# Queries and keys turned by DMA transposes of the sync queue in place of TensorE transposes, in a hybrid transformer block

## The chip, the core and the metric

The kernel runs on one core of a Trainium2 chip. The metric is the device time of one execution in microseconds (us); the median of three executions of the kernel before is 1248.1 us. PE is TensorE, ACT is ScalarE, DVE is VectorE, POOL is GpSimd and SP is the sync engine, whose queue issues all of this kernel's transfers.

## What is computed

One transformer block works on 1024 latent tokens (a grid of 16 x 64) and 256 context tokens, all of width 1024. A modulated norm is projected, and the columns go to three mixers: a Hyena long convolution, grouped-query attention (GQA: 8 query heads, 2 key heads) and neighbourhood attention (4 heads, windows of 8 x 16). An output projection and a SwiGLU network follow. The change touches what lies between the projection and the two attentions:

```python
q_l = apply_rope(rms_norm(q_l, qk_g_q[l]), cos, sin)
k_l = apply_rope(rms_norm(k_l, qk_g_k[l]), cos, sin)
k_c = rms_norm(k_c, qk_g_k[l])
gqa_l = gqa_latent(q_l, jnp.concatenate([k_c, k_l], axis=1),
                   jnp.concatenate([v_c, v_l], axis=1))
na_l = natten_latent(nq_l, nk_l, nv_l, nk_c, nv_c, na_rpb[l])
```

## The kernel before

The kernel is written by hand: five instruction streams, one for each engine, tied by semaphores. Nothing reorders them, so the order in the code is the order on each engine, and a wait holds back everything behind it on that engine. Precise products are made of fp16 pairs: a value is split into a high part (written by ACT) and a low part (written by DVE or POOL), and three matmuls stand for one.

The projection for attention is cut into 28 units of 128 tokens. Units 0 to 9 (group 2) give the neighbourhood keys and values of the 8 latent and 2 context tiles. Units 10 to 19 (group 1) give the GQA keys and values of the 2 context tiles (10, 11) and of the 8 latent tiles (12 to 19); the latter also give the neighbourhood queries. Units 20 to 27 (group 0) give the GQA queries Q of the 8 latent tiles.

A unit u of group 1 goes this way: PE projects it (`project`, 24 matmuls of 512 columns); ACT squares and copies (`from_psum`); DVE sums; POOL takes the inverse root (`inverse_roots`); DVE scales and rotates; ACT writes the high parts into the staging tile `stk[u % 2]` (`hi_parts`), DVE the low parts (semaphore `pr_lo`); then PE turns the staging tile into PSUM, one 128 x 128 transpose for each head (`turn_qk`), and ACT copies the turned tile from PSUM to its home (`turned`, semaphore `pr_tc`). Keys go to `kT`, Q to `qT`; the neighbourhood queries are dealt into blocks of 8 rows x 16 columns in `nqT` by two copies. PE turns unit u - 2 right behind the projection of unit u.

From unit 19 on, neighbourhood attention runs in 32 iterations k (4 heads x 8 query blocks): `scores(k)`, `weigh(k - 2)`, `turn_p(k - 1)` (five fp32 transposes of probabilities) and a quarter of the projection of one Q unit (6 matmuls, `project_q`). In one of four iterations PE also turns a Q unit (8 transposes). `scores(0)` needs the blocked queries of units 12 to 15, `scores(4)` those of 16 to 19. The last Q unit, 27, is turned in GQA, six steps after its start. In some iterations a `chunk` of early GQA scores (512 columns) is added.

SP loads, in this stretch, copies of the neighbourhood values within SBUF (`load_near`, four DMAs of 128 KB each time, 2 then 0 and 1 then 3), bias pieces of 512 KB (`load_bias`), the gates and the next weights.

Of the kernel before, what the change touches and what calls it, by code (L numbers as in the profile page):

```python
# [14 lines left out]
P = 128  # L15
# [320 lines left out]
NKT = NT + NC  # L336
# [3 lines left out]
CATCH_UP, TURN_AT = (3, 6), 5  # L340
# [60 lines left out]
def build(nc, io, cst, lay, out):  # L401
    ctx = ExitStack()
    with ctx:
# [111 lines left out]
        nkT = f16(Z + 67, HN, 2, S + C)  # L515
        nT = [f32(o, 512) for o in (Z + 49, Z + 51)]
# [116 lines left out]
        pr_tc = sem("qk_transposed_copied")  # L633
        near_in = [sem("near_values_in"), sem("last_near_values_in")]
# [105 lines left out]
        def turned_bank(u):  # L740
            if u == NU - 1:
                return OUT_BANK[1]
            if u == GROUP0[0] - 1:
                return turned_bank(u - 1)
            return ((5, 4), (4, 3), (2, 3))[UNITS[u][0]][u % 2]

        def work(u):
            return u % 2

# [129 lines left out]
        def _(sp):  # L879
# [75 lines left out]

            sp.wait_ge(late_used, 2 * CHUNKS.count("late"))
            sp.wait_ge(pr_vl, n_valued(GROUP0[1] - 1))
            load_near(2)
            for n in range(BIAS_EARLY):
                load_bias(n)  # L960
            sp.wait_ge(split_lo, n_split(chunk_index("qkv", 5)))
            for cw in range(2):
                load_near(cw)
            sp.wait_ge(pr_r, n_normed(GROUP0[0] - 1))
            load_near(3)
            sp.wait_ge(pr_mm, GROUP0[0])
# [10 lines left out]
            for n in range(BIAS_EARLY + BIAS_RING, 3 * HN):  # L977
                load_bias(n)
# [141 lines left out]
        def _(pool):  # L1120
# [68 lines left out]

            def rotate_q(u):  # L1190
# [19 lines left out]
            for u in range(GROUP0[1], GROUP0[0]):  # L1210
# [7 lines left out]
                inverse_roots(u)  # L1218
            own.step(pool.memset(shifts, 0.0))
            for u in range(GROUP0[0], NU):  # L1220
# [5 lines left out]
                if u == GROUP0[0] + 2:  # L1226
                    pool.wait_ge(pr_tc, GROUP0[0] + 1)
# [97 lines left out]
        def _(pe):  # L1325
# [241 lines left out]
            def project_q(u, i):  # L1567
# [4 lines left out]
                elif i == 0:  # L1572
                    pe.wait_ge(pr_tc, u - 1)
# [5 lines left out]
            def turn_qk(u):  # L1579

                g, t = UNITS[u]
                pe.wait_ge(pr_lo, u + 1)
                if u == GROUP0[0] - 1:
                    pe.wait_ge(pr_tc, u)
                elif u >= 2:
                    pe.wait_ge(pr_tc, u - 1)
                if u == NU - 1:
                    pe.wait_ge(o_rdy, NNA)
                elif u > GROUP0[0]:
                    pe.wait_ge(s_max, max(n_chunked(Step(n)) for n, k in EARLY.items() if free_bank(k)[0] == u))  # L1590
                out16 = PS[:, turned_bank(u), :].bitcast(F16)
                for j in range(4 if g == 1 and t >= NT else 8):
# [15 lines left out]
            for u in range(2, GROUP0[0] - 1):  # L1608
# [10 lines left out]
                turn_qk(u - 2)  # L1619
# [56 lines left out]
            def chunk(c):  # L1676
# [11 lines left out]
                elif c.s == len(EARLY) + 1:  # L1688
                    pe.wait_ge(pr_tc, NU - 1)
# [1896 lines left out]
```

## Time and profile before

| what | value |
|---|---|
| times of three executions | 1247.28, 1248.1, 1249.35 us |
| span of the profiled execution | 1246.6 us |
| PE busy | 1226.5 us (98%) |
| DVE, ACT, POOL busy | 979.6, 653.0, 398.3 us |
| granted clock of TensorE, mean | 0.998 |
| projection of the units of group 1 | about 229 to 281 us from the span's start |
| iterations of neighbourhood attention | about 271 to 383 us |
| GQA | up to about 550 us |

The span is the time from the first to the last instruction of the profiled execution. It lies 0.7 to 2.8 us under the timed executions, which hold the launch too; the profiled execution has no other time of its own. A matmul's end is modelled, so the start of the next one tells more than a busy share.

### The profile page before, as it was taken

Reading aid. Unit: us, or ns where it says so; the run is one execution under the profiler, and the core shown is the slowest. Engines: PE = TensorE matmul, PEld = TensorE weight load, DVE = VectorE, ACT = ScalarE, POOL = GpSimd, SP = SyncE. Lnnn points to the kernel's source line nnn. Section 1 sums busy time; section 2 is a strip of 40 time slices with the busy share of each in tenths; the row PEclk is TensorE's granted clock in tenths of the full one; section 3 lists DMA queues with packets and bytes.
Section 4 is the critical chain, followed back from the end, with each engine's and each line's share of the span. In section 5 each row is a group of like instructions: output and inputs, shape, how many; then the busy total and the mean of one; then the engine's idle time right before and its main releaser. Section 6 shows DMA issues by size and latency. Waiting matters only on the chain. (4 is left out here: it accounts for less than half of the span.)

```text
span 1246.6 us, 22702 instructions
## 1 busy us (share of the span) xinstructions
PE 1226.5 (98%) x8085; PEld 668.1 (54%) x8085; DVE 979.6 (79%) x1597; ACT 653.0 (52%) x1231; POOL 398.3 (32%) x385
## 2 busy tenths in 40 slices
PE   7999999999999999999999999999999999999998
PEld 1564656556775666664454555554555554444444
DVE  3879998676778999964479888888888885666587
ACT  2642234556779999963145554455555543412425
POOL 0000000114678988850320444445554430000001
PEclk9999999999999999999999999999999999999999
DMA  9728723235210130121300332322223307997963
GB/s 354 282 87 318 260 78 136 68 87 155 67 35 2 35 136 9 29 86 51 118 34 1 102 102 84 92 85 66 87 90 101 101 28 265 336 339 249 351 228 135
DMA packets 111043, 164.35 MB, mean 132 GB/s; under 512 B 8560, under 2 KB 70000, under 8 KB 109552
## 3 DMA queue, kind: packets, MB, share of 16 engines
q1 hardware_dynamic: 110960, 163.24, 38.5%
q8 instruction: 52, 0.85, 0.3%
q14 instruction: 31, 0.25, 0.1%
HBM read 138.57 MB, written 22.55 MB: 129 GB/s over the span
## 5 line engine op out<-in xcount | busy, mean ns | idle before, releaser
L1327 PE MATMUL PS<-arena 128*128 128x512 f16 (+9 forms) x7485 | 1185.2, 319 | 13.1 <-DMA arena<-in_w_mod 5.7
L1327 PEld LDWEIGHTS PS<-arena 128*128 128x128 f16 (+3 forms) x7485 | 617.3, 100 | 555.3 <-issue 33.5
L3133 DVE SCALAR_TENSOR_TENSOR arena<-arena 128x512 f16<-128x512 f32 x128 | 111.6, 878 | 30.6 <-ACT arena L2361 29.8
L2361 ACT ACTIVATE arena<-arena 128x512 f16<-128x512 f32 x120 | 75.4, 631 | 103.2 <-PE PS L1327 103.2
L2491 ACT ACTIVATE arena<-arena 128x512 f16<-128x512 f32 x77 | 48.1, 629 | 124.7 <-DVE arena L3354 74.6
L3017 DVE TENSOR_REDUCE arena<-PS 128x1 f32<-128x512 f32 (+1 forms) x160 | 106.8, 680 | 3.3 <-PE PS L1327 3.3
L1321 POOL TENSOR_TENSOR arena<-arena 128x1 f32<-128x1 f32 x8 | 4.7, 598 | 231.3 <-DVE arena L3521 227.9
L2262 ACT ACTIVATE arena<-PS 128x512 f16<-128x512 f32 x125 | 75.7, 605 | 2.8 <-PE PS L1327 1.8
L1171 POOL TENSOR_TENSOR arena<-arena 128x512 f16<-128x512 f32 x64 | 74.0, 1158 | 8.0 <-ACT arena L2265 5.4
L3190 DVE TENSOR_TENSOR arena<-PS,arena 128x256 f32<-128x256 f32 (+1 forms) x100 | 55.2, 553 | 25.9 <-PE PS L1327 25.6
L3369 DVE SCALAR_TENSOR_TENSOR arena<-arena 128x512 f16<-128x512 f32 x77 | 52.2, 687 | 18.9 <-ACT arena L2491 18.8
L3041 DVE TENSOR_TENSOR arena<-PS,arena 128x512 f16<-128x512 f32 x96 | 65.3, 680 | 1.1 <-ACT PS L2265 0.9
L1297 POOL TENSOR_TENSOR arena<-arena 128x256 f32<-128x256 f32 x10 | 7.3, 726 | 183.7 <-DMA arena<-in_w_ffn_in 183.7
L3354 DVE TENSOR_TENSOR arena<-arena 128x512 f32<-128x512 f32 x44 | 30.2, 691 | 38.6 <-DMA arena<-in_w_ffn_out 33.3
L2436 ACT CAST arena<-arena 128x512 f16<-128x512 f32 (+1 forms) x77 | 45.2, 613 | 29.1 <-DVE arena L3239 17.4
L3253 DVE TENSOR_TENSOR arena<-arena 128x512 f16<-128x512 f32 (+1 forms) x77 | 60.3, 807 | 0.0
L2265 ACT ACTIVATE PS<-PS 128x512 f32<-128x512 f32 x96 | 57.9, 603 | 0.6 <-PE PS L1327 0.6
L1213 POOL MEMSET arena<- 128x128 f16 x2 | 0.4, 205 | 162.4 <-PE PS L1593 162.4
L2406 ACT COPY arena<-PS 128x512 f32<-128x512 f32 x60 | 33.9, 581 | 34.6 <-DVE arena L3253 18.8
L3142 DVE SCALAR_TENSOR_TENSOR arena<-arena 128x512 f16<-128x512 f32 (+2 forms) x30 | 41.6, 1414 | 0.0
L1187 POOL TENSOR_TENSOR arena<-arena 128x2 f32<-128x2 f32 (+1 forms) x18 | 20.3, 1126 | 61.8 <-DVE arena L2870 61.8
L2987 DVE CUSTOM_DVE_ANT_0 PS<-PS,arena 128x640 f32<-128x640 f32 x32 | 26.6, 831 | 17.1 <-PE PS L1327 17.1
(227 smaller groups left out, 1321.0 us busy)
## 6 DMA issues: line engine op xcount, KB each, us to landing
arena<-in_w_ffn_out SPq DMA_DIRECT2D x121, 256.0 KB, 5.2
arena<-in_w_mod SPq DMA_DIRECT2D x23, 1024.0 KB, 7.2
arena<-in_w_ffn_in SPq DMA_DIRECT2D x88, 256.0 KB, 3.0
left_operands<-arena SPq DMA_DIRECT2D x43, 256.0 KB, 2.9
arena<-in_w_in SPq DMA_DIRECT2D x9, 1024.0 KB, 5.6
arena<-left_operands SPq DMA_DIRECT2D x3, 2816.0 KB, 12.1
arena<-lay_bias SPq DMA_DIRECT2D x12, 512.0 KB, 3.9
arena<-in_x SPq DMA_DIRECT2D x2, 2048.0 KB, 14.1
```

The costliest lines, as they stand in the source:

```text
L1171: pool.tensor_tensor(pt[:, 1], Pf[s.full], pt[:, 0], ALU.subtract).then_inc(pt_lo2, 1)
L1327: return pe.matmul(out, lhsT, rhs, start=start, stop=stop, skip_group_check=True)
L2262: act.activation(Pt[s.s % RING_P][:, 0], PS[:, s.bank], ACT.Exp)
L2265: act.activation(Pf[s.full] if s.by_pool else PS[:, s.bank], PS[:, s.bank], ACT.Exp).then_inc(s_exp, 1)
L2361: act.activation(block_split(p, b)[:, 0], weight_block(p, b, first), ACT.Copy, scale=WS).then_inc(blk_hi, 1)
L2491: act.activation(foS[q % FO_RING][:, 0], src, ACT.Copy, scale=WS).then_inc(fo_hi, 1)
L3017: dve.tensor_reduce(out, ps, AX, ALU.max).then_inc(s_max, 1)
L3041: dve.tensor_tensor(pt[:, 1], PS[:, s.bank], pt[:, 0], ALU.subtract).then_inc(pt_lo, 1)
L3133: dve.scalar_tensor_tensor(dst[:, 1], src, WS, dst[:, 0], ALU.mult, ALU.subtract).then_inc(blk_lo, 1)
L3190: dve.tensor_tensor(buf, psum, buf, ALU.add).then_inc(fi_sum, 1)
L3253: dve.tensor_tensor(dst[:, 1], f_op[name], dst[:, 0], ALU.subtract).then_inc(fi_lo, 1)
L3369: dve.scalar_tensor_tensor(foS[q % FO_RING][:, 1], src, WS, foS[q % FO_RING][:, 0], ALU.mult, ALU.subtract).then_inc(fo_lo, 1)
```

## The change

Units 10 to 27 are no longer turned by PE. SP issues a DMA transpose from the staging tile for each: one of [128 x 512] for the keys of a unit of group 1, a second one of [128 x 512] for its neighbourhood queries (units 12 to 19), one of [128 x 1024] for a Q unit. Keys and Q land in `kT` and `qT` at once, without a copy by ACT. The neighbourhood queries land in one staging tile `nq_rows`, and POOL deals them into `nqT` by two copies (`block_queries`). Completion is counted on two semaphores used earlier for loads, `cols_in` and `rest_in`, by the parity of the unit. `pr_tc` now counts `turned` of units 0 to 9 and then `block_queries`. Units 0 to 9 are turned by PE as before.

```diff
+            def turn_qk(u):
+
+                g, t = UNITS[u]
+                sp.wait_ge(pr_lo, u + 1)
+                done = qk_in[u % 2]
+                if g == 0:
+                    sp.dma_start_transpose(qT[:, :, tok(t)], stk[work(u)]).then_inc(done, 16)
+                    return
+                keys = kT.rearrange("p h a s -> p (h a) s")
+                sp.dma_start_transpose(keys[:, :, tok(t)], stk[work(u)][:, 0:512]).then_inc(done, 16)
+                if t < NT:
+                    if t:
+                        sp.wait_ge(pr_tc, u - 2)
+                    sp.dma_start_transpose(nq_rows, stk[work(u)][:, 512:1024]).then_inc(done, 16)
...
-            for n in range(BIAS_EARLY + BIAS_RING, 3 * HN):
-                load_bias(n)
+            pieces = {BiasPiece(n - BIAS_RING).units_done: n for n in range(BIAS_EARLY + BIAS_RING, 3 * HN)}
+            for v in range(NNA):
+                if v % 4 == 3 and v > 3:
+                    turn_qk(GROUP0[0] + v // 4 - 1)
+                if v in pieces:
+                    load_bias(pieces[v])
+            turn_qk(NU - 1)
...
+            def block_queries(u):
+
+                t = UNITS[u][1]
+                pool.wait_ge(*qk_turned(u))
+                for r in range(2):
...
+                    ins = pool.tensor_copy(dst, nq_rows[:, :, GRID_W * r:GRID_W * r + GRID_W]
+                                           .rearrange("p h (b c) -> p h b c", b=4))
+                ins.then_inc(pr_tc, 1)
...
                 inverse_roots(u)
+                if u - 2 >= GROUP0[1] + NC:
+                    block_queries(u - 2)
...
-                elif i == 0:
-                    pe.wait_ge(pr_tc, u - 1)
+                elif i == 0 and u >= GROUP0[0] + 2:
+                    pe.wait_ge(pr_n, n_normed(u - 2))
...
                 project(u)
-                turn_qk(u - 2)
+                if u - 2 < GROUP0[1]:
+                    turn_qk(u - 2)
...
-            pe.wait_ge(pr_tc, GROUP0[1] + NC + NT // 2)
+            pe.wait_ge(pr_tc, GROUP0[1] + NT // 2)
             scores(Unit(0))
...
                 if k == 4:
-                    pe.wait_ge(pr_tc, first)
+                    pe.wait_ge(pr_tc, GROUP0[1] + NT)
...
-                if q_unit(k, 5) is not None:
-                    turn_qk(q_unit(k, 5))
...
-                if u >= 2:
+                if u >= GROUP0[1] + 2:
+                    act.wait_ge(*qk_turned(u - 2))
+                elif u >= 2:
...
-            if s == TURN_AT + 1:
-                turned(NU - 1)
```

How it moves the SP queue between the end of the weight loads and the gates. Before, `32x4x512` is one DMA of a near load and `lay_bias` a bias piece:

```order
L945 DMA arena<-arena 32x4x512 [waits values_lo,late_product_added]
L945 DMA arena<-arena 32x4x512 x3
L953 DMA arena<-lay_bias 128x1024 x2
L945 DMA arena<-arena 32x4x512 [waits split_lo]
L945 DMA arena<-arena 32x4x512 x7
L945 DMA arena<-arena 32x4x512 [waits qk_rotated]
L945 DMA arena<-arena 32x4x512 x3
```

The same stretch of the change, from the key transpose of unit 13 (its first row) to the keys of unit 17:

```order
L972 DMA_TRANSPOSE arena<-arena 128x4x128 [waits qk_lo]
L976 DMA_TRANSPOSE arena<-arena 128x4x128 [waits qk_transposed_copied]
L952 DMA arena<-arena 32x4x512 [waits values_lo,late_product_added]
L952 DMA arena<-arena 32x4x512 x3
L960 DMA arena<-lay_bias 128x1024 x2
L972 DMA_TRANSPOSE arena<-arena 128x4x128 [waits qk_lo]
L976 DMA_TRANSPOSE arena<-arena 128x4x128 [waits qk_transposed_copied]
L972 DMA_TRANSPOSE arena<-arena 128x4x128 [waits qk_lo]
L976 DMA_TRANSPOSE arena<-arena 128x4x128 [waits qk_transposed_copied]
L952 DMA arena<-arena 32x4x512 [waits split_lo]
L952 DMA arena<-arena 32x4x512 x7
L972 DMA_TRANSPOSE arena<-arena 128x4x128 [waits qk_lo]
```

The two transposes of units 14 and 15 stand between the near loads, those of units 16 to 18 behind the second batch, those of unit 19 behind the last; each second one (L976) waits for POOL to have emptied `nq_rows`.

On POOL, before, the inverse roots of units 12 to 19 (L1187) stand in a row, then a memset of `shifts` and the root of unit 20:

```order
L1216 MEMSET arena 128x16
L1216 MEMSET arena 128x4
L1187 TENSOR_TENSOR arena<-arena 128x2 [waits qk_mean_square,pool_steps] x8
L1219 MEMSET arena 128x512
L1187 TENSOR_TENSOR arena<-arena 128x8 [waits qk_mean_square]
```

The change, from the root of unit 18 on (L1222 is the root, L1233 the blocking copies, `columns_in` and `rest_in` the completion of a transpose of an even and of an odd unit):

```order
L1222 TENSOR_TENSOR arena<-arena 128x2 [waits qk_mean_square,pool_steps]
L1233 COPY arena<-arena 128x4x4x16 [waits columns_in]
L1233 COPY arena<-arena 128x4x4x16
L1222 TENSOR_TENSOR arena<-arena 128x2 [waits qk_mean_square,pool_steps]
L1233 COPY arena<-arena 128x4x4x16 [waits rest_in]
L1233 COPY arena<-arena 128x4x4x16
L1233 COPY arena<-arena 128x4x4x16 [waits columns_in]
L1233 COPY arena<-arena 128x4x4x16
L1233 COPY arena<-arena 128x4x4x16 [waits rest_in]
L1233 COPY arena<-arena 128x4x4x16
L1271 MEMSET arena 128x512 [waits qk_transposed_copied]
```

From the root of unit 14 on, each root is followed by a wait for the transfer of the unit two before and its two copies (unit 16 behind the root of 18), and the last root by those of units 17, 18 and 19.

## Rows read from the trace of the kernel before

**Rows 1.** The page: busy time of the engines, and TensorE's granted clock by slices.
```profile
PE 1226.5 (98%) x8085; PEld 668.1 (54%) x8085; DVE 979.6 (79%) x1597; ACT 653.0 (52%) x1231; POOL 398.3 (32%) x385
PEclk9999999999999999999999999999999999999999
```
**Rows 2.** Windows: length; PE, PEld, DVE, ACT, POOL busy us; clock; DMA share; GB/s.
```profile
230.00:281.00 51.00, 50.92 (x314) 26.90 (x312) 33.06 (x104) 27.90 (x75) 6.89 (x12) 1.00 0.28 78
299.00:375.00 76.00, 75.35 (x838) 53.21 (x835) 57.69 (x151) 57.06 (x140) 51.62 (x45) 1.00 0.21 67
387.00:430.00 43.00, 41.69 (x509) 27.36 (x507) 40.89 (x73) 42.59 (x85) 35.87 (x43) 1.00 0.09 26
```
**Rows 3.** Timeline of PE in group 1 (start, length, operation): projections and turns.
```profile
234.49 0.39 PE L1593 MATMUL PS<-arena 128*128 128x128 f16 x4
234.72 5.34 PE L1327 MATMUL PS<-arena 128*128 128x512 f16 x24
...
256.55 0.61 PE L1593 MATMUL PS<-arena 128*128 128x128 f16 x8
257.00 5.34 PE L1327 MATMUL PS<-arena 128*128 128x512 f16 x24
262.18 0.61 PE L1593 MATMUL PS<-arena 128*128 128x128 f16 x8
...
281.14 0.62 PE L1593 MATMUL PS<-arena 128*128 128x128 f16 x8 [0.22 <-DVE arena L2923]
```
**Rows 4.** Timeline of PE, one period of four near iterations.
```profile
299.23 0.61 PE L1593 MATMUL PS<-arena 128*128 128x128 f16 x8
...
303.24 0.74 PE L1656 MATMUL PS<-arena 128*128 128x128 f32 x5
303.81 2.66 PE L1327 MATMUL PS<-arena 128*128 128x512 f16 x28
306.31 0.74 PE L1656 MATMUL PS<-arena 128*128 128x128 f32 x5
...
311.81 0.61 PE L1593 MATMUL PS<-arena 128*128 128x128 f16 x8
```
**Rows 5.** Timeline of PE, near iterations with neither turn nor chunk.
```profile
283.44 0.72 PE L1656 MATMUL PS<-arena 128*128 128x128 f32 x5
284.00 2.44 PE L1327 MATMUL PS<-arena 128*128 128x512 f16 x27
286.28 0.74 PE L1656 MATMUL PS<-arena 128*128 128x128 f32 x5
```
**Rows 6.** Timeline of ACT at the start of GQA.
```profile
387.62 1.02 ACT L2170 COPY arena<-PS 128x1024 f16<-128x1024 f16 x1
```
**Rows 7.** Timeline of SP's issues, merged: near loads and bias pieces.
```profile
255.84 2.70 SPq L945 DMA_DIRECT2D arena<-arena  x4
258.59 1.07 SPq L953 DMA_DIRECT2D arena<-lay_bias  x2
262.17 5.13 SPq L945 DMA_DIRECT2D arena<-arena  x8
...
278.98 2.52 SPq L945 DMA_DIRECT2D arena<-arena  x4
```
**Rows 8.** The line of the near loads: issue ns, and us from issue to landing.
```profile
L945 SPq DMA_DIRECT2D arena<-arena x16: 586/604/750, 255.8 to 280.9; - x16
...
DMA to landing us min/median/max: 2.3/2.4/2.5
```
**Rows 9.** Copies like the blocking: lines of POOL and ACT, ns min/median/max.
```profile
L1159 POOL COPY arena<-arena x16: 601/604/609, 323.0 to 530.7; 64x512 f16<-64x512 f16 x16
L1213 POOL MEMSET arena<- x2: 205/205/205, 226.5 to 229.5; 128x128 f16 x2
L2185 ACT COPY arena<-PS x16: 372/384/490, 249.0 to 282.5; 128x256 f16<-128x256 f16 x16
```
**Rows 10.** Timeline of the weight loads of PE before `scores(4)`.
```profile
288.40 1.05 PEld L1327 LDWEIGHTS PS<-arena 128*128 128x128 f16 x21 [0.58 <-issue]
```
**Rows 11.** Timeline of PE and ACT at the longest pause of this stretch.
```profile
294.67 0.77 ACT L2239 ACTIVATE arena<-PS 128x384 f16<-128x384 f32 x2 [1.15 <-remote]
295.81 1.16 PE L1327 MATMUL PS<-arena 128*128 128x384 f16 x21 [1.50 <-issue]
```

More of the change, by code:

```diff
@@ L339 @@
 LEAD, LAG, SHIFT_AT, SEND_AT = 13, 4, 8, 4
-CATCH_UP, TURN_AT = (3, 6), 5
+CATCH_UP = (3, 6)
 RING_P, RING_F = 5, 4
@@ L515, in build @@
         nkT = f16(Z + 67, HN, 2, S + C)
+        nq_rows = f16(101.5, HN, P)
         nT = [f32(o, 512) for o in (Z + 49, Z + 51)]
@@ L740, in turned_bank, with has_q, qk_turned @@
         def turned_bank(u):
[L741 to L745, printed above, removed]
+            return 2 + u % 2
         def work(u):
             return u % 2
+        def has_q(u):
+            g, t = UNITS[u]
+            return g == 0 or (g == 1 and t < NT)
+        def qk_turned(u):
+            n = sum(2 if UNITS[v][0] == 1 and has_q(v) else 1 for v in range(GROUP0[1], u + 1) if v % 2 == u % 2)
+            return qk_in[u % 2], (16, N_REST)[u % 2] + 16 * n
         def q_unit(k, after):
@@ L954, in load_bias @@
                     .then_inc(bias_in[piece.slot], 16)
+            def turn_qk(u):
+                g, t = UNITS[u]
+                sp.wait_ge(pr_lo, u + 1)
[9 more added lines that the diff above has]
+                    sp.dma_start_transpose(nq_rows, stk[work(u)][:, 512:1024]).then_inc(done, 16)
+            sp.wait_ge(y_rdy, 4)
+            for u in range(GROUP0[1], GROUP0[1] + 4):
+                turn_qk(u)
             sp.wait_ge(late_used, 2 * CHUNKS.count("late"))
@@ L960, in _ @@
                 load_bias(n)
+            for u in range(GROUP0[1] + 4, GROUP0[1] + 6):
+                turn_qk(u)
             sp.wait_ge(split_lo, n_split(chunk_index("qkv", 5)))
@@ L963, in _ @@
                 load_near(cw)
+            for u in range(GROUP0[1] + 6, GROUP0[0] - 1):
+                turn_qk(u)
             sp.wait_ge(pr_r, n_normed(GROUP0[0] - 1))
             load_near(3)
+            turn_qk(GROUP0[0] - 1)
             sp.wait_ge(pr_mm, GROUP0[0])
@@ L1218, in _ @@
                 inverse_roots(u)
+                if u - 2 >= GROUP0[1] + NC:
+                    block_queries(u - 2)
+            for u in range(GROUP0[0] - 2, GROUP0[0]):
+                block_queries(u)
+            pool.wait_ge(pr_tc, GROUP0[1] + NT)
             own.step(pool.memset(shifts, 0.0))
@@ L1579, in turn_qk @@
             def turn_qk(u):
-                g, t = UNITS[u]
                 pe.wait_ge(pr_lo, u + 1)
-                if u == GROUP0[0] - 1:
-                    pe.wait_ge(pr_tc, u)
-                elif u >= 2:
+                if u >= 2:
                     pe.wait_ge(pr_tc, u - 1)
[L1587 to L1590, printed above, removed]
                 out16 = PS[:, turned_bank(u), :].bitcast(F16)
-                for j in range(4 if g == 1 and t >= NT else 8):
+                for j in range(8):
                     ins = pe.transpose(out16[:, j * P:j * P + P], stk[work(u)][:, j * P:j * P + P], ident16)
@@ L1688, in chunk @@
                 elif c.s == len(EARLY) + 1:
-                    pe.wait_ge(pr_tc, NU - 1)
+                    pe.wait_ge(s_max, n_chunked(Step(NKT)))
+                    for u in (NU - 3, NU - 2):
+                        pe.wait_ge(*qk_turned(u))
                 else:
@@ L1774, in _ @@
             weigh(Unit(0))
-            turn_qk(first - 1)
             project_q(first, 2)
@@ L2223, in _ @@
                 hi_parts(u - 1)
-                turned(u - 2)
+                if u - 2 < GROUP0[1]:
+                    turned(u - 2)
             def exponentials(u):
@@ L2286, in _ @@
             from_psum(first - 1)
-            turned(first - 3)
             copy_p(Unit(0))
-            turned(first - 2)
             hi_parts(first - 1)
             exponentials(Unit(1))
-            turned(first - 1)
             for k in range(2, NNA):
@@ L2295, in _ @@
                     from_psum(q_unit(k, 1))
-                if q_unit(k, 5) is not None:
-                    turned(q_unit(k, 5))
                 if k > 2:
```

38 lines of the change are left out of this document (13 added, 25 removed).

## The prediction

> **What bounds the kernel now.** The page first: PE is busy 98% of the span at a granted clock of full speed throughout, 2.4 GHz [rows 1]. That is an average, so I read the stretches that the change touches by windows: in the projections of group 1 PE is busy 50.92 of 51 us while DVE, ACT and POOL have room; in the iterations of neighbourhood attention 75.35 of 76; in early GQA ACT is fullest, 42.59 of 43 [rows 2]. The timeline of PE then shows what a turn costs, by starts. In group 1 one unit takes 5.63 us (256.55 to 262.18), of which eight transposes hold 0.45 (256.55 to 257.00), four 0.23 [rows 3]. So this stage goes at PE's pace, and a transpose taken from PE comes off the end if nothing else gets late.
>
> **What the change removes.** Group 1: units 12 to 19 lose 8 transposes each, 10 and 11 four: 8 x 0.45 + 2 x 0.23 = 4.0 us, and the wait of 0.22 in front of the turn of unit 19 [rows 3]: 4.2.
>
> Near iterations: a period of four takes 12.58 us (299.23 to 311.81). Two of its iterations have a chunk and no turn and take 3.07 (303.24 to 306.31) [rows 4]. What an iteration with neither takes is seen ahead of the first Q turn: 2.84 (283.44 to 286.28) [rows 5]. A period without the turn, and without the wait for ACT's copy of it, is then 2 x 3.07 + 2 x 2.84 = 11.82: 0.76 less. I take 0.73, for 7 turns: 5.1.
>
> Unit 27: 0.45 us of PE and a copy of 1.02 us on ACT [rows 6], which sets the pace there. Nothing below 0, at most 1.0; I take 0.7, since DVE with 40.89 of 43 follows closely [rows 2]. Sum of gains: 4.2 + 5.1 + 0.7 = 10.0 us.
>
> The copies that ACT loses in group 1 are counted at nothing: ACT is busy 27.9 of 51 us there [rows 2], and it waits for PE. The sixteen POOL copies are hidden in themselves (POOL has 6.89 of 51), as long as their data is there.
>
> **What it adds: one chain.** `nq_rows` is a single tile. So the query transpose of unit u can't start before POOL has blocked unit u - 1, and that not before its transfer has landed. Behind SP's wait stand the near loads, bias pieces and gates; behind POOL's wait the inverse root of unit u + 3, on which PE's next projection but one depends; behind ACT's wait in `hi_parts` the next exponentials. From unit 14 on the chain runs without slack, and `scores(4)` on PE waits for its end, unit 19 blocked. Let D be the time SP needs to issue a transpose, L that from the start of the issue to the landing, and B the blocking of one unit.
>
> B: two copies of 256 elements a partition. POOL's memset of 128 elements takes 0.205 us, its copy of 512 takes 0.604, ACT's copy of the same shape 0.384 [rows 9]. I take 0.4 each and 0.3 for two hand-overs: 1.1.
>
> D and L are not in this trace. Lower end: the near loads also move 128 KB within SBUF; they issue in 0.604 us and land after 2.4 [rows 8]. Upper end: if the four 128 x 128 blocks were pushed one by one like the four DMAs of a near load, D = 2.7 [rows 7], and L = 2.1 + 2.4 = 4.5 (the last of four starts 2.70 - 0.60 later). I take D = 0.65 and L = 3.0, nearer to the copy of the same size and route; above it because each follows another transpose or a near load in the same queue.
>
> The chain in the clock of the old trace: SP is done with the first near load and two bias pieces at 258.59 + 1.07 = 259.66 [rows 7]; what releases it, DVE's last accumulation, follows PE's projections, and PE is ahead by 0.9 by then (the turns of 10, 11 and 12: 0.23 + 0.23 + 0.45), so 258.8. Keys of 14 (D), its queries (L), B: the queries of 15 start at 259.9 + D + L. Behind their issue SP issues eight near DMAs (5.13 [rows 7]) and the keys of 16: the queries of 16 start at 265.0 + 3D + L. Three more steps of L + 1.1 lead to those of 19 (the third is 2D + 2.52 if that is longer, for the last near load stands in it [rows 7]), and L + 1.1 to the end: 269.4 + 3D + 5L = 286.4.
>
> PE's weight loads for `scores(4)` start at 288.40 [rows 10]; with 4.2 us less work ahead PE is there at 284.2. The stall is 5L - 12.9 at D = 0.65: **2.1 us**. `scores(0)` waits for unit 15 of the same chain earlier (ready at 259.9 + D + 2L + 1.1 = 267.7); a stall there is no extra term, since the chain doesn't wait for PE and the later stall contains it.
>
> What a page says here can be left out without loss. The Trainium skill ("DMA: Bandwidth & Descriptors", Latency and other measured facts) gives a DMA transpose 261 GB/s at worst; 128 KB would then flow in an estimated 0.5 us, and L would lie near the lower end: stall 0, time 1238.1. No run here shows it yet.
>
> The Q units' transposes I count at nothing. SP can issue that of unit 20 when its low part is written, before iteration 7, where PE turned it; its first use is the chunk of iteration 9, two iterations of 2.8 to 3.1 us later [rows 4, 5], and L = 3.0 fits in. The others have a whole period of four iterations each. If that cover went (L over 6), PE would wait before a chunk, and a bias piece queued behind the transpose would be late.
>
> **Sum.** Gains 10.0, stall 2.1: 7.9 less. The profiled execution spans 1246.6, and would span 1238.7; the median of the timed runs is 1.5 more than the span, 1248.1, so the forecast is **1240.2 us**. A measurement of this kernel tells about 0.2%, 2.5 us, from no change.
>
> **The rivals.**
> 1. *Slower: transposes pushed block by block.* The place is the same chain, before `scores(4)`. With D = 2.7 and L = 4.5 the third step becomes 2D + 2.52 = 7.9: 265.0 + 8.1 + 4.5 + 5.6 + 5.6 + 7.9 + 5.6 = 302.3, a stall of 18.1 and 1256.2 us. It decides from a stall of 10.0 on, that is L = 4.6 at D = 0.65. For it: a near load shows that four issues in a row hold SP for 2.5 to 2.7 us [rows 7], and sixteen transposes share that queue. Against it: the order has each as one instruction on SP. Chance 0.20. By the Trainium skill ("VectorE: DVE Perf Modes", The three transpose paths) a 128 x 128 transpose takes 1309 ns by DMA and 390 on TensorE, and it advises TensorE where PSUM will do; four in a row are an estimated 5.2 us, the stall 13.1 and the time 1251.2. The trace disagrees on the side of PE: 0.45 us for eight, 56 ns each [rows 3].
> 2. *No stall.* L = 2.4 as for the near loads: the gains alone, 1238.1. Chance 0.17.
> 3. *The ring holds the near iterations.* If an iteration without a turn takes 3.07 whether it has a chunk or not, because DVE's low part of the probabilities comes when it comes, the period is 12.28, the gain 7 x 0.30 = 2.1 instead of 5.1, and the time 1243.2. The row of 2.84 speaks against it [rows 5], but it is from before the chunks begin. Chance 0.15.
> 4. *Nothing to measure.* L between 4.1 and 5.1: gain and stall within 2.5 us of each other, about 1248. Chance 0.12.
> The forecast itself (stall 0.5 to 4.5, 1238.5 to 1242.5) has 0.36.
>
> One pause I can't place: ACT stops 1.15 us and PE 1.50 at 294 to 296 with no work named as the cause [rows 11]. It may go or move; it widens the low end by up to 1.5 and is no term.
>
> **The numbers.** Faster by over 0.2%: 0.36 + 0.17 + 0.15 = 0.68. Within: 0.12. Slower: 0.20. The range reaches from 1237, a part of the pause below rival 2, to 1249.5, most of rival 4, and leaves the slow rival out.
>
> **What would show it.** In the changed profile: no 128 x 128 fp16 transposes after unit 9, and a unit of group 1 in 5.2 us; near periods of about 11.8 (12.3 by rival 3); transposes landing about 3.0 us after issue; PE idle about 2 us before the fifth near scores, released by POOL's blocking copy; ACT without the 1.02 copy in GQA. The prediction is wrong if L is over 4, or if POOL's or ACT's wait for a transfer delays PE elsewhere.

## The result, and the profile after

The changed kernel takes 1253.2 us at the median against 1248.8 for the kernel before beside it: ratio 1.0032, 95% interval 1.0022 to 1.0042. It is slower, by 0.3%; the forecast was 1240.2 and faster. Its profiled execution spans 1251.3 us, 4.7 more than that of the kernel before.

The page: TensorE has less to do than before [rows 1], 1222.7 us, and still the end is later. So the question is where it waits, or runs slowly.

```profile
PE 1222.7 (98%) x7949; PEld 662.0 (53%) x7949; DVE 980.2 (78%) x1597; ACT 637.2 (51%) x1197; POOL 404.5 (32%) x401
PE   8999999987999999999999999999999999999998
```

The second row gives PE's busy share in tenths for 40 slices of the span. It has one dent that the kernel before has not, slices 9 and 10 (250 to 313 us). The timeline of PE in that stretch (start, length, operation; in brackets the idle time just before and what ended it):

```profile
269.62 7.58 PE L1379 MATMUL PS<-arena 128*128 128x384 f16 x30 [2.53 <-POOL arena L1233]
277.04 0.71 PE L1704 MATMUL PS<-arena 128*128 128x128 f32 x5
...
282.09 2.44 PE L1379 MATMUL PS<-arena 128*128 128x64 f16 x27 [1.21 <-DVE arena L3019]
...
290.51 1.16 PE L1379 MATMUL PS<-arena 128*128 128x256 f16 x21 [1.27 <-POOL arena L1233]
...
305.32 2.01 PE L1379 MATMUL PS<-arena 128*128 128x512 f16 x12
312.10 1.41 PE L1379 MATMUL PS<-arena 128*128 128x512 f16 x16 [4.77 <-DMA arena<-arena]
313.32 1.31 PE L1704 MATMUL PS<-arena 128*128 128x128 f32 x5
314.42 4.28 PE L1379 MATMUL PS<-arena 128*128 128x512 f16 x28
318.53 0.74 PE L1704 MATMUL PS<-arena 128*128 128x128 f32 x5
...
324.31 0.74 PE L1704 MATMUL PS<-arena 128*128 128x128 f32 x5
...
336.23 0.74 PE L1704 MATMUL PS<-arena 128*128 128x128 f32 x5
```

Each row of L1704 is the turn of one unit's probabilities, and so a clock for the iterations. Three things are to be seen. `scores(0)` waits 2.53 us for GpSimd's block copies (L1233); two shorter waits follow, 1.21 us for low parts (L3019) and 1.27 before `scores(4)`. The chunk of iteration 9 waits 4.77 us for a DMA, and what follows is slow: 4.28 us for 28 matmuls, where [rows 4] has 2.66. And from there on the gain of the forecast is there: a period of four iterations takes 336.23 - 324.31 = 11.92 us, 12.58 before [rows 4].

The sync queue's issues in the same stretch (L972 keys, L976 neighbourhood queries, L969 Q units, L952 near loads, L960 bias, L1002 gates, L904 w_out; the length is the time SP needs to issue them):

```profile
254.93 2.68 SPq L952 DMA_DIRECT2D arena<-arena  x4
257.65 1.08 SPq L960 DMA_DIRECT2D arena<-lay_bias  x2
258.77 1.41 SPq L972 DMA_TRANSPOSE arena<-arena  x1
260.23 1.26 SPq L976 DMA_TRANSPOSE arena<-arena  x1
...
274.43 1.26 SPq L976 DMA_TRANSPOSE arena<-arena  x1
...
289.59 1.40 SPq L1002 DMA_DIRECT2D gates<-arena  x2
292.19 2.79 SPq L904 DMA_DIRECT2D arena<-in_w_out  x2
299.46 7.57 SPq L969 DMA_TRANSPOSE arena<-arena  x1
```

And the three lines of transposes (ns of an issue, min/median/max; us from issue to landing, min/median/max):

```profile
L972 SPq DMA_TRANSPOSE arena<-arena x10: 1190/1304/1602, 232.9 to 284.9; - x10
DMA to landing us min/median/max: 2.4/2.6/6.2
L976 SPq DMA_TRANSPOSE arena<-arena x8: 1188/1258/1267, 244.7 to 286.2; - x8
DMA to landing us min/median/max: 2.4/2.5/5.2
L969 SPq DMA_TRANSPOSE arena<-arena x8: 1232/1239/7567, 299.5 to 391.4; - x8
DMA to landing us min/median/max: 3.0/3.0/12.6
```

A transpose lands at the median after 2.5 to 3.0 us, as forecast or sooner. The maxima belong to the two long waits of PE: unit 14's pair (5.2 and 6.2 us, behind a near load and two bias pieces) and Q unit 20's (12.6, behind gates and w_out; 7.57 of it SP stood in the issue).

**My theory** from these rows: the price of a transpose was about right, and the loss is the place of two of them in the one queue, with TensorE's clock behind each wait. **Rivals:** two dependent pairs are too slow for this chain wherever they stand; of gates and w_out only one is in the way; a wait removed comes back further on.

### The profile page after: what moved, and what is told of

The parts are those of the page before. It is cut to its first block, busy times and chain, and to the rows that moved or that the text cites. A ratio compares the mean times of both kernels' runs of the same rounds, so it can differ in the third digit from the quotient of the medians.

```text
span 1251.3 us, 22426 instructions
## 1 busy us (share of the span) xinstructions
PE 1222.7 (98%) x7949; PEld 662.0 (53%) x7949; DVE 980.2 (78%) x1597; ACT 637.2 (51%) x1197; POOL 404.5 (32%) x401
## 4 chain that ended last, share of the span: by engine, by line
PE 65%; DVE 4%; DMA 3%; issue 3%; ACT 2%; POOL 2%; SPq 1%; POOLq 0%; ACTq 0%; DVEq 0%
PE PS L1379 63%; DMA arena<-arena 2%; PE PS L1704 1%; DMA arena<-weight_sum_rows 1%; DVE arena L3477 1%; DVE arena L3480 1%; SPq L952 1%; PE PS L1454 1%; ACT arena L2562 1%; ACT PS L2295 1%; DVE arena L3040 0%; POOL arena L1206 0%; ACT arena L2295 0%; ACT arena L2290 0%; POOL arena L1233 0%
## 5 line engine op out<-in xcount | busy, mean ns | idle before, releaser
L2295 ACT ACTIVATE arena<-PS 128x512 f32<-128x512 f32 x64 | 38.6, 603 | 0.2 <-PE PS L1379 0.2
```

The costliest lines, as they stand in the source:

```text
L2295: act.activation(Pf[s.full] if s.by_pool else PS[:, s.bank], PS[:, s.bank], ACT.Exp).then_inc(s_exp, 1)
```

## The experiments

Ratios are to the kernel before, run on the same chip, with the 95% interval. The runs come from four chips, on which the kernel before takes 1248.4 to 1249.8 us, so that ratios compare better than times.

| run | edit | us | ratio |
|---|---|---|---|
| e1 | changed kernel, unit 14 first | 1249.1 | 0.9995 (0.9985 to 1.0005) |
| e2 | changed kernel, gates late | 1250.5 | 1.0012 (1.0002 to 1.0022) |
| e3 | changed kernel, w_out late | 1244.9 | 0.9969 (0.9957 to 0.9981) |
| e4 | e1, e2 and e3 | 1246.6 | 0.9981 (0.9970 to 0.9992) |
| e5 | e1 and e3 | 1242.4 | 0.9943 (0.9930 to 0.9957) |
| e14 | e5 again | 1241.7 | 0.9940 (0.9925 to 0.9956) |
| e6 | e5, unit 16 before near 0 and 1 | 1244.7 | 0.9958 (0.9944 to 0.9972) |
| e11 | e5, unit 19 before near 3 | 1245.1 | 0.9967 (0.9955 to 0.9979) |
| e7 | changed kernel, PE busy in the wait | 1251.7 | 1.0016 (1.0007 to 1.0026) |
| e10 | kernel before, w_out held | 1247.7 | 0.9993 (0.9984 to 1.0002) |
| e8 | group 1 by DMA alone, unit 14 first | 1249.1 | 1.0000 (0.9988 to 1.0011) |
| e9 | e8, w_out held | 1249.1 | 1.0000 (0.9991 to 1.0009) |
| e12 | e9 without a guard of its own | 1246.7 | 0.9981 (0.9970 to 0.9992) |
| e13 | Q units by DMA alone, w_out late | 1244.8 | 0.9962 (0.9950 to 0.9974) |

**e1: unit 14's transposes first.**

```diff
-            for u in range(GROUP0[1], GROUP0[1] + 4):
+            for u in range(GROUP0[1], GROUP0[1] + 5):
                 turn_qk(u)
...
             load_near(2)
...
-            for u in range(GROUP0[1] + 4, GROUP0[1] + 6):
-                turn_qk(u)
+            turn_qk(GROUP0[1] + 5)
```

> Edit: in the sync queue the two transposes of unit 14 are issued ahead of the four transfers of near-values window 2 and the first two bias pieces; nothing else moves. My theory (the transposes themselves cost about what was forecast, the loss lies in where they stand in the one queue): in the changed kernel unit 14's transposes were issued at 258.8 and 260.2 us, landed 5.2 to 6.2 us later, and scores(0) waited 2.53 us for their block copies, after which TensorE's granted clock stood at 0.50. Issued at about 254 and 255 us they land in 2.4 to 3 us, scores(0) no longer waits more than 0.3 us, the clock stays above 0.9 there, and 2.5 + 1.8 us are saved at that place; what of it is still there at the end 2.5 to 4.3, so 1249 to 1251 us. Rival 1 (a chain of two dependent pairs of transposes is too slow by itself, wherever it stands): scores(0) still waits 1.5 us or more, 1252 to 1253 us. Rival 2 (a pause only moves): scores(0) starts on time and the same time is lost before scores(4) or chunk 0, 1253 us.

The issues of SP, and the timeline of PE:

```profile
253.95 1.19 SPq L972 DMA_TRANSPOSE arena<-arena  x1
```
```profile
267.74 5.90 PE L1378 MATMUL PS<-arena 128*128 128x384 f16 x30 [0.30 <-POOL arena L1232]
273.48 0.71 PE L1703 MATMUL PS<-arena 128*128 128x128 f32 x5
```

The wait is 0.30 us instead of 2.53, and the same 30 matmuls take 5.90 instead of 7.58. By windows (length; PE, PEld, DVE, ACT, POOL busy; clock; DMA share; GB/s), the changed kernel and then e1:

```profile
270.00:272.00 2.00, 2.00 (x9) 1.01 (x8) 1.71 (x8) 0.44 (x2) 0.26 (x1) 0.50 0.69 166
```
```profile
270.00:272.00 2.00, 2.00 (x11) 0.91 (x10) 0.91 (x6) 0.89 (x2) 0.00 (x0) 1.00 0.79 160
```

In the changed kernel the granted clock is at half after the wait, in e1 at full. 0.37% of the time comes back, 4.6 us, the first turn of probabilities 3.56 earlier (277.04 to 273.48). The theory holds for this place; both rivals fall. But e1 moves the whole chain of transposes too: `scores(4)` starts at 287.37 in it and at 290.51 in the changed kernel. So it doesn't tell what the fall of the clock costs by itself; e5 and e14 do, below.

**e2 and e3: gates late, or w_out late.** In e2 the two gates transfers go behind the last w_out loads; in e3 the first two w_out loads go behind unit 20's transpose:

```diff
-            for n in range(2):
-                load(chunk_index("wo", n), w_out[:, 0:4, 512 * n:512 * n + 512], (4, 512))
...
                     turn_qk(GROUP0[0] + v // 4 - 1)
+                    if v == 7:
+                        for n in range(2):
+                            load(chunk_index("wo", n), w_out[:, 0:4, 512 * n:512 * n + 512], (4, 512))
```

> Edit: the two transfers that write the gates to DRAM four bytes at a time go from ahead of the first two w_out loads to behind the last two, some 90 us later; w_out stays ahead of Q unit 20's transpose. Theory A (the small writes hold up everything behind them in the queue): the w_out loads, issued at 292, move at once and land by about 302 to 304 instead of 308; unit 20's transpose is issued at about 299.5 in 1.3 us instead of 7.57 and lands by 305, before chunk 0 asks at 307.3; the wait of 4.77 us in iteration 9 and the half clock after it (2 to 3.3 us) go: 1245 to 1247 us. Theory B (the 2 MB of w_out alone hold it up): the transpose's landing moves by less than 2 us and chunk 0 still waits 3 us or more: 1251 to 1253 us.

> Edit: the two w_out loads (1 MB each) are issued behind Q unit 20's transpose instead of ahead of it; the gates stay where they are. Theory A (the small writes hold up the queue until about 303): the transpose, issued at 299.5 in 1.3 us, still lands only at 303 to 306, so chunk 0 waits no more or less than 1 us, and the landing from the issue is over 3.5 us: 1245 to 1247 us. Theory B (w_out alone is in the way): it lands within 3 us of its issue, by 302.5, and the time is the same 1245 to 1247 us; the landing tells them apart here, the time in the run before. Against both: if the transposes from the 8 Q units are slow whatever stands ahead (their landings 3.0 at the median), chunk 0 waits over 2 us and the time stays above 1250. A cost of the edit: w_out lands some 8 us later, at about 310 to 313, where GpSimd first scales it at about 310, so GpSimd may wait 3 us with slack behind it.

The issues of SP in e2, then in e3:

```profile
292.60 0.94 SPq L904 DMA_DIRECT2D arena<-in_w_out  x2
299.81 1.27 SPq L969 DMA_TRANSPOSE arena<-arena  x1
```
```profile
289.27 1.13 SPq L1002 DMA_DIRECT2D gates<-arena  x2
299.80 1.27 SPq L969 DMA_TRANSPOSE arena<-arena  x1
```

And the DMA view of 298 to 301 us (KB each where it is known, us to landing) of the changed kernel, e2 and e3:

```profile
arena<-arena SPq DMA_TRANSPOSE x1, 12.6
```
```profile
arena<-arena SPq DMA_TRANSPOSE x1, 5.1
```
```profile
arena<-arena SPq DMA_TRANSPOSE x1, 6.2
```

By the landings theory A holds in both runs (304.9 in e2, 6.2 us after the issue in e3) and B in neither; but A is not the whole, for with the gates left in place w_out's move alone ends the wait too. The same transpose, issued at the same time, lands after 5.1 us with w_out ahead of it, 6.2 with the gates ahead and w_out right behind, 12.6 with both ahead; PE asks 7.9 us after the issue (299.46 to 305.32 + 2.01). So either move ends the wait. How much of 5.1 and 6.2 is due to what stands ahead, the two runs don't show: in e4, where neither does and w_out comes right behind, the transpose of unit 20 is issued at 295.83 and lands after 4.8. In the changed kernel w_out itself took 16.1 us to land, in e2 8.1: the small writes hold up what follows, and 2 MB more then stands ahead of the transpose. The Trainium skill ("DMA: Bandwidth & Descriptors", Queues, rings and completion order) says that each DMA engine takes the descriptors of a ring in order, and (Specifications) that transfers under 512 B are not moved at line rate. The trace agrees. The DMA view of 286 to 312 us, its packets in the changed kernel and in e2, and the changed kernel's GB/s in 40 slices of 0.65 us:

```profile
GB/s 197 73 145 49 21 101 284 403 353 422 410 397 47 3 13 13 41 16 28 13 38 25 32 44 50 25 50 57 161 381 388 403 425 365 381 333 141 43 173 427
DMA packets 5821, 4.53 MB, mean 174 GB/s; under 512 B 4320, under 2 KB 4347, under 8 KB 5818
```
```profile
DMA packets 3831, 4.80 MB, mean 185 GB/s; under 512 B 2256, under 2 KB 2292, under 8 KB 3828
```

The gates make some 2060 packets under 512 B (4320 - 2256), and from slice 13 to 28 (293.8 to 304.2 us), with w_out waiting, the queue moves 3 to 57 GB/s.

e3 gave the time that was expected (0.1 us under its range), e2 did not. Up to the last turn of probabilities it is as early as e3 (375.4 and 375.3, 383.9 in the changed kernel), but the gates now stand in another place, issued at 451.8, and there the timelines of DVE, ACT and PE show:

```profile
465.72 0.69 DVE L3040 TENSOR_REDUCE arena<-PS 128x1 f32<-128x512 f32 x1 [4.81 <-remote]
465.68 0.60 ACT L2290 ACTIVATE arena<-PS 128x512 f16<-128x512 f32 x1 [4.78 <-remote]
466.46 8.82 PE L1379 MATMUL PS<-arena 128*128 128x512 f16 x86 [3.92 <-DVE arena L3040]
```

Two engines stop for 4.8 us, for something that the trace calls remote, and the clock is at 0.73 of full from 465 to 470.

**e4 and e5: the moves together.**

> Edit: the three moves at once (unit 14's transposes first, gates behind the last w_out loads, first w_out loads behind Q unit 20's transpose). If the whole loss is the order of the sync queue and the clock that falls after the two pauses, the parts add up: 1253.2 less 2.5 to 4.3 less 6 to 8 is 1241 to 1245 us, faster than the kernel before by 0.3 to 0.6%, and no wait of TensorE over 1.3 us is left between 262 and 330 us. Rival: the two moves of the queue relieve the same few us once, because the next wait (scores(4), 1.27 us; the low parts that VectorE writes, 1.0 to 1.2 us) takes it up: 1246 us or more.

> Edit: the changed kernel with unit 14's transposes first and the first w_out loads behind Q unit 20's transpose; the gates keep their place (moved behind the last w_out loads they cost about 4 us near 460 us in the run of all three). Theory: the two stalls are separate, so the savings add: the run with w_out moved alone gave 1244.9 us and still had the 2.34 us wait before scores(0) and the half clock behind it, together some 3.6 to 4 us (turn of unit 0's probabilities at 277.7 there, at 273.4 with unit 14 first): 1240.5 to 1241.5 us, 0.6% under the kernel before. Rival: what is gained at scores(0) is waited for again before scores(4) and chunk 0, and the time stays at 1244 to 1245.

In e4 no wait over 1.3 us is left from 262 to 330, and the last turn of probabilities starts at 371.4, 12.5 earlier than in the changed kernel. Of that the span of its profiled execution keeps 8.7; behind the gates' late place DVE stops there for 3.03 us at 457. The profiled execution took 1244.4 us; the median of e4, 1246.6, is over the 1241 to 1245 expected and where the rival put it. e5 leaves the gates where they were: 0.57% under the kernel before, 0.9 us over the range expected. Against the changed kernel e1 gives 0.37%, e3 0.63%, both together 0.89%: they nearly add up. What is left to wait for in e5 on PE:

```profile
267.45 5.90 PE L1379 MATMUL PS<-arena 128*128 128x384 f16 x30 [0.54 <-POOL arena L1233]
278.60 2.44 PE L1379 MATMUL PS<-arena 128*128 128x64 f16 x27 [1.56 <-DVE arena L3019]
287.01 1.16 PE L1379 MATMUL PS<-arena 128*128 128x256 f16 x21 [1.27 <-POOL arena L1233]
303.61 0.83 PE L1379 MATMUL PS<-arena 128*128 128x512 f16 x16 [0.17 <-DMA arena<-arena]
```

e14 is the same kernel once more. In its profile the clock is at half behind `scores(0)`:

```profile
268.12 7.33 PE L1379 MATMUL PS<-arena 128*128 128x384 f16 x30 [1.34 <-POOL arena L1233]
279.63 2.44 PE L1379 MATMUL PS<-arena 128*128 128x64 f16 x27 [0.49 <-DVE arena L3019]
```

Its first turn of probabilities starts 2.1 us later than e5's (275.29 against 273.19), `scores(4)` 0.9 later (287.90), and the last turn of probabilities no later (372.55 against 372.68). The next wait is shorter by 1.07, and the rest goes into later waits of e5 too. So time lost at `scores(0)` is taken out of the waits that follow, as long as the chain of transposes sets their ends.

**e6 and e11: two more transposes ahead of near loads.** `turn_qk(16)` before `load_near(0)` and `load_near(1)`; `turn_qk(19)` before `load_near(3)`.

> Edit: the run before this one, and also unit 16's transposes ahead of the eight transfers of near-values windows 0 and 1, which take 5.5 us to issue. Theory: with unit 14 first, unit 16's key transpose was issued at 269.6 in the moment when those eight were out, so the chain of units 16 to 19 stands behind them; some 5 us earlier it ends the waits of 1.2 to 1.3 us (ScalarE held up by unit 17's landing, seen as VectorE's low parts) and 1.2 to 1.6 us before scores(4): another 1 to 2.5 us less, 1238.5 to 1240.5 us. Rival: the chain is set by its own landings and by the projections, and the windows then come late for the first weighing at 278: no gain, or up to 1 us more than the run before this one.

> Edit: the run with unit 14 first and w_out late, and also unit 19's transposes ahead of the four transfers of near-values window 3. Theory: scores(4) waited 1.27 us at 287.0 there for the block copies of unit 19, whose query transpose was issued at 282.7 behind those four (2.55 us of the queue) though the blocks before it were done at 280.8; issued at about 281 it ends that wait, 0.5 to 1.3 us less: 1241 to 1242 us. Rival: window 3 then lands later than the fifth unit's weighing wants it, and as with unit 16 ahead of windows 0 and 1 (1244.7) the time goes up by 1 us or more.

Both rivals hold in their direction: 0.15% and 0.24% more than e5, though both intervals overlap e5's. ACT in e6 and in e11, at the first `scaled`, which in the program waits for near window 3:

```profile
286.64 0.31 ACT L2278 ACTIVATE arena<-PS,arena 128x64 f32<-128x64 f32 x1 [3.42 <-issue]
```
```profile
288.36 0.31 ACT L2277 ACTIVATE arena<-PS,arena 128x64 f32<-128x64 f32 x1 [4.64 <-issue]
```

Window 3 is issued at 278.78 in e5, at 280.98 in e6 and at 283.39 in e11. PE waits 2.50 and 3.73 us behind ACT, more than the 1.3 to 1.6 that were to be won. So in e6 it is not windows 0 and 1 that come too late, as its rival had it, but window 3 behind them. In both the 30 matmuls behind the wait of `scores(0)` also took 7.59 us instead of 5.90 by the clock, after waits as short as e5's (0.46 and 0.62 us); e14 had as much and ended no later, so I don't put the difference down to it.

**e7: TensorE kept busy in the wait.**

```diff
                 if early_chunk(k) == 0:
+                    pe.wait_ge(pr_n, n_normed(free_bank(k)[0]))
+                    for _ in range(22):
+                        mm(PS[:, chunk_bank(Step(0)), :], ident16, nkT[:, 0, 0, 0:512], True, True)
                     pe.wait_ge(*qk_turned(first))
```

> Edit: the changed kernel as it is, and in front of TensorE's wait for Q unit 20's transpose 22 further matmuls of 128 by 512 into the bank that chunk 0 overwrites (their products are not used), about 4.7 us of work at full clock in place of 4.77 us of pause. The landing at 312.1 stays where it is. Theory (the clock falls because of the pause): the granted clock stays over 0.95 from 311 to 319 where it was 0.58, the iteration after the wait takes 3.1 us instead of 5.21, and 2 to 3 us are saved: 1250.3 to 1251.3 us. Rival (the half clock has nothing to do with the pause, or the time behind it is the transfers' doing): 1253 us, or more by what the added matmuls delay.

Windows of PE (length; busy; clock; DMA share; GB/s), the changed kernel and then e7:

```profile
311.00:313.00 2.00, 0.90 (x11) 0.50 0.97 322
313.00:315.00 2.00, 2.00 (x17) 0.50 0.00 0
```
```profile
311.00:313.00 2.00, 1.20 (x6) 1.00 0.64 175
313.00:315.00 2.00, 1.73 (x24) 1.00 0.42 166
```

With work in place of the pause the clock stays at full, and the iteration behind it takes 3.07 us (turns at 313.94 and 317.01) instead of 5.21. The landing came 1.2 us later here (the wait ends at 313.27), and still the time is 0.16% lower, 2.0 us (1251.7, 0.4 over the range expected). So the half clock is the pause's doing and costs 2 us or more at this place, behind which the iterations of TensorE follow each other without waits.

**e8 to e10, e12 and e13: the halves of the change.** e8 is the changed kernel with unit 14 first and the Q units back on TensorE; e9 holds w_out until unit 20's low part is there; e10 does that alone in the kernel before; e12 is e9 without a wait that I had put in as a guard, in front of the projection of a Q unit; e13 is the kernel before with the Q units by DMA.

```diff
+            sp.wait_ge(pr_lo, GROUP0[0] + 1)
             for n in range(2):
                 load(chunk_index("wo", n), w_out[:, 0:4, 512 * n:512 * n + 512], (4, 512))
```
```diff
-                elif i == 0:
-                    pe.wait_ge(pr_tc, max(u - 1, GROUP0[0]) - NC)
+                elif i == 0 and u >= GROUP0[0] + 2:
+                    pe.wait_ge(pr_tc, u - 1 - NC)
```

> Edit: keys and neighbourhood queries are turned by DMA as in the changed kernel with unit 14's transposes first, and the Q units are turned by TensorE and copied by ScalarE as in the kernel before. It measures the two halves of the change apart. From the traces: with unit 14 first the first turn of probabilities starts 2.7 us earlier than in the kernel before, and the waits up to scores(4) give back some of it, while the iterations of the near part keep the 12.58 us for four of the kernel before: 1245.5 to 1248 us, and 4 to 5.5 us above the run with unit 14 first and w_out late, which is then the worth of the Q units' half without its stall. Rival: the Q units' half is worth nothing (the period is set elsewhere), and this run equals that one within 1 us.

> Edit: the run with group 1 by DMA, unit 14 first and the Q units on TensorE, and in it the first two w_out loads held until the low parts of unit 20 are there, as in the run that moved them behind unit 20's transpose. That run without this (1249.1 us) had waits of TensorE of 3.2 and 3.3 us at 288 and 303, the second behind VectorE and ScalarE, which waited 4.5 and 3.7 us for something outside the program's own work while the gates' small writes and w_out were on their way; the runs with w_out late show no such wait. Theory: without it this run gives 1245 to 1247.5 us, group 1's half is worth 1 to 3 us and the Q units' half, by the difference to 1242.4, 3 to 5. Rival: group 1's half is worth nothing, and the time stays at 1248 to 1249.5 us.

> Edit: the kernel before, with the first two w_out loads held until the low parts of unit 20 are there, and nothing else. It is the control for the runs with w_out late: how much of their gain has nothing to do with the transposes. In the kernel before ScalarE waited 1.15 us and TensorE 1.50 us at 294 to 297 while gates and w_out were on their way. Theory: that pause goes, 1 to 1.5 us less, about 1247 to 1248 us, so most of what w_out late gave the changed kernel (8.4 us) is unit 20's wait and what followed it. Rival: w_out late is worth 3 us or more to the kernel before as well, and the gain of the changed kernel with both moves (0.57%) shrinks by as much.

> Edit: the run with group 1 by DMA, Q units on TensorE and w_out held, without the wait for the last block copies that the projection of unit 21 had in it (2.43 us at 288, with the clock at 0.84 behind it). Theory: group 1's half has the gain of the forecast (4.2 us of turns) less the waits that are left (scores(0) 0.5 to 1.4, low parts 0.5 to 1.5, scores(4) 1.3) and, where the clock falls, 1.3 more: worth 0 to 2 us over the kernel before with w_out held (1247.7), so 1245.7 to 1247.7 us. Rival: it stays at 1249, and group 1's half is a loss by itself.

> Edit: the kernel before with only the Q units' half of the change: their transposes from the sync queue, the first w_out loads behind unit 20's; keys and neighbourhood queries are turned by TensorE as before. Theory: the near part's iterations go from 12.58 to 11.9 us for four, seven times, as forecast, and unit 27's turn goes: 4.5 to 5.5 us under the kernel before with w_out held (1247.7), so 1242 to 1243.5 us, as fast as both halves together. Rival: both halves are needed (without group 1 by DMA ScalarE or the chunk banks hold the near part up), 1245 us or more; or group 1's half is worth its 2 us and both together stay 2 us ahead.

> Edit: none; the run with unit 14 first and w_out late once more, on the chip of the two others, so that halves and whole are compared there. 1241.9 to 1243.5 us.

e8 and e9 missed what I expected, and by themselves would have said that group 1's half is worth nothing (e8's profile, with its stops of 3.7 and 4.5 us, is of an execution of 1252.3 us, 3.3 over its median). The rows of PE in e9 and e12 show why:

```profile
287.97 4.14 PE L1376 MATMUL PS<-arena 128*128 128x512 f16 x27 [2.43 <-POOL arena L1230]
```
```profile
287.16 1.16 PE L1376 MATMUL PS<-arena 128*128 128x256 f16 x21 [1.37 <-POOL arena L1230]
```

In e9 PE stands with 27 matmuls to do, the projection of unit 21 among them, which my guard tied to the last block copies; in e12 that projection is done before it waits. The clock from 288 to 299 is 0.84 in e9 and 1.00 in e12. Against the kernel before with w_out held (0.9993), group 1's half is worth 0.12% (1.5 us; the intervals overlap, so by itself it is not certain), the Q units' half 0.31% (3.9 us), both 0.5 to 0.53% (6.2 to 6.6). By the medians both are needed for the whole; the intervals of e13 and e14 still overlap. And w_out late is worth at most 0.2% to the kernel before (interval), but 0.63%, 7.9 us, to the changed one: nearly all of that is unit 20's wait and what followed it. The pause of [rows 11] did not go in e10 as I had expected (ACT 2.7 us, PE 1.29). e13 came out 1.3 us above its estimate, 0.6 by the ratio, since the kernel before took longer on that chip; its profile has a wait of ACT of 3.4 us of the kind seen in e2, and one of PE of 2.01 behind it.

## Why the prediction was wrong

By its own steps, the changed kernel's trace against the forecast:

| step | forecast | measured |
|---|---|---|
| turns of group 1 | 4.2 us | of 2 x 0.23 + 6 x 0.45 = 3.2 up to the first turn of probabilities, 2.7 came with 0.3 of wait (e1); the rest is taken as forecast |
| a near period | 0.73 less | 0.66 less, seven times 4.6 |
| unit 27 | 0.7 | 0.2 (4.89 late at the last turn of probabilities, 4.7 at the end) |
| D, B | 0.65, 1.1 us | 1.24 to 1.30 at the medians; 0.74 to 0.84 for the two copies |
| L | 3.0 | 2.5 (Q units 3.0) at the median; 5.2, 6.2 and 12.6 behind other transfers |
| stall up to `scores(4)` | 2.1 | 6.7 in four parts, the next rows |
| of it `scores(0)` | in the 2.1 | 2.53, and 7.58 - 5.90 = 1.7 by the clock |
| of it low parts (L3019) | no term | 1.21, ACT standing in `hi_parts` for a landing |
| of it `scores(4)` | 2.1 | 1.27 |
| Q unit 20 | nothing | 4.77; by the clock 8.58 - 3.08 - 4.77 = 0.7 in its own iteration (turns of probabilities at 304.74 and 313.32) and 5.21 - 3.08 = 2.1 in the next |

The gains are 4.2 + 4.6 + 0.2 = 9.0, the losses 6.7 + 7.6 = 14.3: 5.3 us slower, where the spans differ by 4.7. Half of the rest is that this profiled execution was 0.3 us ahead before the stretch began (its projection of unit 12 starts at 228.99, at 229.31 in the kernel before). Waits of 0.42 and 1.04 us at 293.97 and 303.75 are not counted: the kernel before has its pause of 1.50 [rows 11].

**The step that failed** is "The Q units' transposes I count at nothing", 7.6 us. It took L = 3.0 for a transfer that has the gates and 2 MB of w_out ahead of it in the same queue, and landed after 12.6. The text names the condition itself ("if that cover went (L over 6)"), and never asked what would stand ahead of unit 20: in the program gates and w_out come just before. e2 and e3 show it: either one moved, no wait. The cover of two iterations was there, 7.9 us; L was not one number but one for each place in the queue.

**The second failing step** is the length of the chain up to `scores(4)`, a stall of 2.1 us that measured 6.7. With L = 3.0 and D = 0.65 the queries of 16 were to be issued at 265.0 + 3D + L = 269.95 and the chain to end at 286.4; they were issued at 274.43, and `scores(4)` starts at 290.51. Of the 4.5 us up to the queries of 16, 2.7 come with unit 14's pair (its landing of 5.2, and D), the rest with D twice more and the near loads. From 284.2, where PE was to be, to 290.51 is 6.3: the waits and the clock together, less the 0.3 by which PE was ahead. So the step "the later stall contains it" held, for the fall of the clock too: e5 and e14 show that, and so do the changed kernel and e3, where the first turn of probabilities starts 0.64 later in e3 (277.68) and the second no later (284.32 against 284.37). What failed is the size of that stall. The text had "wrong if L is over 4" as a sign, and took one L for all places here too.

**What held:** the gains of group 1 and of the near part (rival 3, the ring, falls: iterations without a chunk go at 2.85 to 2.92), and that four blocks are not issued one by one (rival 1 falls: D is 1.25, not 2.7, and the slow end came by another way). On the estimate of 5.2 us from "VectorE: DVE Perf Modes" in the Trainium skill the trace disagrees: four blocks of 128 by 128 land in 2.5, eight in 3.0. D was put at half of what it is; what that cost was in part won back, since with L smaller the chain's step is 3.3 us (queries of units 16, 17 and 18 issued at 270.94, 274.24 and 277.54 in e5) where 4.1 was forecast.

With the queue in order (e5, e14) the change gives 0.57 to 0.60%, 7.1 to 7.5 us, where 7.9 was forecast; up to 2 us of it, 0.9 by the middle of e10's interval, w_out late may give without the change. That this lies so near is in part luck: in e5's profile PE waits 3.4 us up to `scores(4)` where 2.1 was forecast, and the pause of 1.50 [rows 11], which the forecast kept, is a wait of 0.64.

## What to carry to other kernels

A transfer's latency depends on its place in the queue: before an engine is made to wait for a DMA, list what is issued ahead of it and right behind it, with bytes and packet sizes, and price it by the landings of those. Put what an engine waits for ahead of loads that nobody needs soon, but move only as far as the loads have slack (e6 and e11 issued near window 3 by 2.2 and 4.6 us later, and TensorE waited 2.5 and 3.7 us behind it). And a pause of TensorE is to be priced with what the clock does after it, here 2.8 us on top of 4.8 at unit 20; but where a chain on other engines ends a later wait anyway, that wait takes the loss up, as at `scores(0)` in e14.

## What the runs showed of the hardware

- Two transfers of 4 KB written four bytes at a time landed after 9.7 to 11.1 us in e3; in the changed kernel, with 2 MB of w_out waiting behind them, the queue moved 3 to 57 GB/s for ten us.
- One and the same transfer, Q unit 20's transpose, landed after 3.5 us (e13: the gates 15.6 us before it, w_out right behind), 4.8 (e4: w_out right behind, no gates), 5.1 (e2: w_out ahead, no gates), 5.3 to 7.6 (e3, e5, e6, e11, e14: gates 9.6 to 12.2 us before, w_out right behind) and 12.0 to 13.7 (changed kernel, e1, e7: gates and w_out ahead; SP stood in the issue for 7.0 to 8.7 of that). In e5 and e6, with 7.5 and 7.6, TensorE waited 0.17 and 0.39 us for it, in the changed kernel 4.77. Over the 3.0 of the later Q units its landing lost 9.6 there, against 2.1 in e2 and 3.2 in e3: the delays did not add.
- Shortly after these writes engines stopped for something that the trace calls remote: ACT 1.15 us in the kernel before [rows 11], 1.5 in the changed kernel and 1.6 in e7, ACT 4.8 and DVE 4.8 in e2, DVE 3.0 in e4, ACT 3.7 and DVE 4.5 in e8, ACT 2.7 in e10 and 3.4 in e13; none up to 500 us in the other eight. That they follow the gates to another place (e2, e4) speaks for the writes as the cause, and against w_out that in e10 and e13 it was issued only after the stop. What is late was not tried, and why e1, e3, e5, e6, e9, e11, e12 and e14 are free of it stays open.
- The granted clock fell to 0.50, that is 1.2 GHz, after waits of 2.5 and 4.8 us. After shorter ones it went either way: full after 0.30, 0.52, 0.54 and 1.12 (e1, e4, e5, e8), lower after 0.46, 0.62 and 0.72 (e6, e11, e12), where the same 30 matmuls took 7.59 us instead of 5.90, and after 1.34 and 1.44 (e14, e9; 7.33 and 7.21). e5 and e14 are one kernel, so it can fall in one profile and not in another; what decides it at these short waits stays open.
